# One more block's index scores in the projection, the attention's order rebuilt on them, split waits between the two stages, and a combination finished by VectorE one tile later

## The chip, the cores and the metric

The kernel is one program on one core of a Trainium2 chip. The core has five engines that run their own instruction streams and meet at semaphores: TensorE (PE; its weight loads are shown apart as PEld), VectorE (DVE), ScalarE (ACT), GpSimd (POOL) and SyncE (SP, which here only issues DMAs). The metric is the device time of one execution in microseconds (us).

## The reference

A decoder layer on 2048 tokens of width 1024, all in float32. Cut to what the change touches:

```python
h = layer_norm(x)
proj = h @ w_in                       # u, q (6 heads), k, v (2 heads), iq (8 index heads), ik, iw
# attention, in blocks of 128 queries
s = einsum('bqhd,bsd->bqhs', iq_block, ik)
idx_score = einsum('bqhs,bqh->bqs', relu(s), iw_block * w_scale)   # then causal
sel = top_k(idx_score, 256)           # softmax attention over the selected keys only
h = layer_norm(ALPHA_RES * h + concat(pool_out, attn_out) @ w_out)
# 32 experts, 4 per token; y are the experts' rows, tok and gates say whose they are
out = zeros.at[tok].add(y * gates)
h = layer_norm(ALPHA_RES * h + out)
```

Block b may see (b + 1) * 128 keys, so the top 256 are a real choice from block 2 on.

## The kernel before

Five stages follow each other, each a block of five instruction streams with a meeting of all engines at its end: projection, attention, placing of tokens on experts, experts, combination.

**Projection** (`project_stage`) walks 16 tiles of 128 tokens. TensorE does 40 matrix products a tile (L527) and, between them, transposes. For the blocks in `SEARCHED` = 2 to 6 it also makes the index scores: two matmuls for a pair of index heads (L498), `rectify` on ScalarE, a weighting matmul (L511), for each chunk of 512 keys. `schedule` says in which tile a block is scored (`score_at` = 3, 4, 6, 8, 11). VectorE then finds the limit of the 256 largest scores by 32 halvings (`search`, a "bit" is one pass L426 over the scores and two small instructions) and makes a mask, which goes to DRAM. ScalarE ends each tile by issuing three DMAs: `qi` (L564), `iw` (L567) and a sixteenth of the zeros that clear the spare rows of `y` (L570). At the end ScalarE waits for the stores of `qi`, `iw` and for `s_clear`, all sixteen clears.

**Attention** (`attend_stage`) walks the 16 blocks in the order `ORDER`, cut into `PHASES`. While the blocks of phase p are worked, VectorE searches block `SEARCHED[p]` (32 bits spread over the heads by `bits`, then `select`), and TensorE and ScalarE make the scores of the next one to be searched, one chunk of 512 keys in a slot (`at_slot`: step, head). Before, the phases were `(0,1,2,3), (4,15), (5,14), (6,13), (12,), (11,), (10,), (9,), (8,), (7,)` and the blocks to be searched 15, 14, 13, ..., 8, 7. Step 0 (block 0) had the four score chunks of block 15 and no search; the search began in step 1. Step 13 (block 9) had the two chunks of block 7, step 14 (block 8) its search, and step 15 (block 7) no search. `walk` sets one order of pieces for every engine: `logits`, `search`, `fill` (score and exponentials), `values`, and work of the two blocks before (`project`, `norm`, `route`, `choose`, `rank`, `scatter`). A block of up to 1024 keys uses half of the `qk` bank (`halved`), so two heads can be under way; a larger one the whole. VectorE and ScalarE began by waiting for all constants (`s_const`, nine DMAs) and, like TensorE, VectorE for all that GpSimd prepares (`s_made` 3).

**Combination** (`combine_stage`) walks 16 tiles. GpSimd gathers the four expert rows of each token with four indirect DMAs a tile (L2051), four tiles ahead (`rows` has four slots). TensorE adds them (L2091 the biases, L2098 the rows) in one of three banks, VectorE adds the residual and takes mean and variance (`sums`: L2126, L2129, L2130, L2132, L2134), GpSimd raises to the power -1/2 (L2068) and makes the shift in two more instructions (L2070, L2072), with a `drain` (wait until the engine's earlier work is done) between them. ScalarE applies scale and shift (L2158), and VectorE multiplies and adds (`affine`: L2139, L2141) one tile later. SyncE stores the tile; `total` has three slots.

Of the kernel before, what the change touches and what calls it, by code (L numbers as in the profile page):

```python
# [27 lines left out]
P = 128  # L28
# [47 lines left out]
def project_stage(nc, A, S, D_):  # L76
# [7 lines left out]
    SHARE = (MAX_VISITS - EXPERTS) * ROWS // TILES  # L84
    SHARE_N = next(n for n in range(1, SHARE + 1) if SHARE % n == 0 and SHARE // n <= P)
    assert SHARE * TILES == (MAX_VISITS - EXPERTS) * ROWS
# [3 lines left out]
    s_keys = [P * (b + 1) for b in SEARCHED]  # L90
    chunks = [-(-n // BANK) for n in s_keys]
    chunk0 = [sum(chunks[:s]) for s in range(len(SEARCHED) + 1)]

    def schedule():
# [4 lines left out]
        for s, b in enumerate(SEARCHED):  # L99
# [48 lines left out]
    with ExitStack() as ctx:  # L148
# [29 lines left out]
        bit_value = sb("bit_value_e", [P, 32])  # L178
        bit_next = sb("bit_next_e", [P, 32], I32)
        scores = sb("scores_e", [P, 2, EARLY * P])  # L180
        mask = sb("mask_e", [P, 2, EARLY * P], BF16)
        causal = sb("causal_e", [P, TOPK // P, TOPK], BF16)
# [3 lines left out]
        same_row = sb("same_row_e", [P, CUT])  # L186
# [23 lines left out]
        s_qst = [sem("p_qst0"), sem("p_qst1")]  # L210
        s_iwst = [sem("p_iwst0"), sem("p_iwst1")]
# [13 lines left out]
        with nc.Block() as block:  # L225
            @block.sync
            def _(sp):
# [7 lines left out]
                def load_queries(s):  # L235
                    b = SEARCHED[s]
# [32 lines left out]
                for b in range(TOPK // P):  # L269
                    sp.dma_start(D_["mask"][b * P:(b + 1) * P, 0:(b + 1) * P], causal[:, b, 0:(b + 1) * P]  # L270
                                 ).then_inc(s_early, 16)
# [22 lines left out]
            def _(pool):  # L294
# [9 lines left out]
                def cut(s):  # L304
                    b = SEARCHED[s]
# [13 lines left out]
                nc.gpsimd.memset(causal[:], 0.0)  # L319
# [9 lines left out]
                for b in range(TOPK // P):  # L329
                    op = nc.gpsimd.affine_select(out=causal[:, b], in_=causal[:, b], compare_op=ALU.is_ge, fill=NEG,  # L330
                                                 base=b * P, pattern=[[-1, TOPK]], channel_multiplier=1)
# [139 lines left out]
            def _(pe):  # L471
# [16 lines left out]
                def index(s, c, i):  # L488
# [3 lines left out]
                    if c == 0 and i == 0:  # L492
                        pe.wait_ge(s_iq, 16 * (s + 1))
                        pe.wait_ge(s_qi, 4 * SEARCHED[s] + 4)
# [43 lines left out]
            def _(act):  # L538
# [6 lines left out]
                def out_of_q(t, g):  # L545
# [15 lines left out]
                    else:  # L561
# [5 lines left out]
                        nc.scalar.dma_start(D_["iw"][t * P:(t + 1) * P, :], iw_now[:, slot]).then_inc(s_iwst[slot], 16)  # L567
                        shape = [SHARE // SHARE_N, SHARE_N * D // P, P]
# [59 lines left out]
                for n in range(2):  # L628
                    act.wait_ge(s_qst[n], 8 * TILES)
                    act.wait_ge(s_iwst[n], 8 * TILES)  # L630
                act.wait_ge(s_clear, 16 * TILES)


def attend_stage(nc, A, S, D_):
# [7 lines left out]
    CONSTS = 16 * 9  # L642
# [7 lines left out]
    PHASES = ((0, 1, 2, 3), (4, 15), (5, 14), (6, 13), (12,), (11,), (10,), (9,), (8,), (7,))  # L650
    SEARCHED = tuple(b for blocks in PHASES for b in blocks if b >= EARLY)
    ORDER = tuple(b for blocks in PHASES for b in blocks)
# [6 lines left out]
    chunks = [-(-n // BANK) for n in s_keys]  # L659
# [4 lines left out]
    for c in range(chunks[0]):  # L664
        at_slot[0, (1, 2, 4, 5)[c]] = (0, c)
    for s in range(1, N_SEARCH):
        steps = [k for k in range(TILES) if PHASE[k] == s - 1 and (s > 1 or k >= 2)]
# [5 lines left out]
    def bits():  # L673
# [3 lines left out]
        for s in range(N_SEARCH):  # L677
            slots = [(k, i) for k in range(TILES) if PHASE[k] == s and (s > 0 or k >= 1) for i in range(HEADS)]
# [19 lines left out]
    def walk(do):  # L698
# [29 lines left out]
        for k in range(TILES + 2):  # L728
# [27 lines left out]
            for s in range(1, N_SEARCH):  # L756
# [8 lines left out]
    with ExitStack() as ctx:  # L765
# [17 lines left out]
        scores = [sb("scores_even", [P, SEQ]), sb("scores_odd", [P, SEQ - P])]  # L783

        band0 = scores[1][:, 0:POOL_GROUPS * P].rearrange("p (g n) -> p g n", n=P)
# [4 lines left out]
        same_row = sb("same_row", [P, CUT])  # L790
# [22 lines left out]
        bit_value = sb("bit_value_sb", [P, 32])  # L813
        bit_next = sb("bit_next_sb", [P, 32], I32)
# [1424 lines left out]
```

## Time and profile before

| | us |
|---|---|
| median of 3 runs (5124.47 to 5127.0) | 5126.84 |
| the profiled execution's own time | 5125.14 |
| its span, first to last instruction | 5123.5 |
| projection, to the first instruction of attention | 602.13 |
| first instruction of the combination | 4888.58 |

TensorE's mean granted clock was 0.933 of full speed. Over the span TensorE was busy 4555.4 us (89%), VectorE 3081.0 (60%), ScalarE 1839.5 (36%), GpSimd 883.7 (17%). How to read the rows below: times are from the start of the span; a line L12 is line 12 of the kernel before; "[9.1 <-X]" is the time the engine stood idle before the instruction and what ended the wait; "issue" there means that no engine or transfer that the profile knows ended it.

### The profile page before, as it was taken

To read this page: it belongs to the slowest core of one execution; us is meant where nothing else is said; L and a number is where in the kernel's file an instruction comes from. 1 tells how busy PE (TensorE), PEld (TensorE's weight loads), DVE (VectorE), ACT (ScalarE), POOL (GpSimd) and SP (SyncE) were. 2 spreads that over 40 slices of the span, in tenths; PEclk is the share of its full clock that TensorE was granted. 3 is DMA by queue.
4 is the path that set the end of the run, shared out by engine and by line. 5 is a ranking of instruction groups with operands and counts; after the bars stand their busy time and mean duration, and the time that the engine had idled before them with its cause. 6 is when DMAs were issued, how large, how long until landed. Compare 5 with 4: busy or idle time off the path is not lost. (4 is left out here: it accounts for less than half of the span.)

```text
span 5123.5 us, 67487 instructions
## 1 busy us (share of the span) xinstructions
PE 4555.4 (89%) x23642; PEld 3404.9 (66%) x23695; DVE 3081.0 (60%) x4864; ACT 1839.5 (36%) x2652; POOL 883.7 (17%) x907
## 2 busy tenths in 40 slices
PE   8999777788888887489999999999999999999953
PEld 4444333344444444289999999999999999999920
DVE  3667445666678885365656655565675566765634
ACT  1222123233333332144444534353454444543411
POOL 0000012111111112221211221121121112211133
PEclk9999788999999898699999999999999999999965
DMA  4323400000000000255454644464565455654465
GB/s 165 122 92 119 135 18 25 16 18 23 12 18 14 21 14 14 99 192 181 176 176 174 227 160 170 161 215 170 174 225 190 164 198 180 220 190 177 141 224 192
DMA packets 523786, 666.09 MB, mean 130 GB/s; under 512 B 57920, under 2 KB 388160, under 8 KB 523616
## 3 DMA queue, kind: packets, MB, share of 16 engines
q1 hardware_dynamic: 400080, 484.90, 27.9%
q10 hardware_dynamic: 96992, 93.93, 5.4%
q0 software_dynamic: 26576, 85.56, 4.6%
q8 instruction: 69, 1.13, 0.1%
q14 instruction: 69, 0.57, 0.0%
HBM read 543.96 MB, written 120.36 MB: 130 GB/s over the span
## 5 line engine op out<-in xcount | busy, mean ns | idle before, releaser
L1767 PE MATMUL gu<-x_hi,w_hi 128*128 128x256 f32 (+2 forms) x4096 | 1229.8, 300 | 1.3 <-DVE x_lo L1849 1.3
L1768 PE MATMUL gu<-x_lo,w_hi 128*128 128x256 f32 (+2 forms) x4096 | 1229.6, 300 | 0.0
L1769 PE MATMUL gu<-x_hi,w_lo 128*128 128x256 f32 (+2 forms) x4096 | 1228.0, 300 | 0.0
L1844 DVE TENSOR_TENSOR w_lo<-w_raw,w_hi 128x2048 fp32r<-128x2048 f32 x386 | 874.6, 2287 | 530.8 <-ACT w_hi L1918 530.8
L1918 ACT ACTIVATE w_hi<-w_raw 128x2048 fp32r<-128x2048 f32 x386 | 726.8, 1907 | 280.6 <-PE gu L1769 198.7
L1767 PEld LDWEIGHTS gu<-x_hi,w_hi 128*128 128x128 f32 x4096 | 770.5, 188 | 2.5 <-issue 1.7
L1769 PEld LDWEIGHTS gu<-x_hi,w_lo 128*128 128x128 f32 x4096 | 771.4, 188 | 0.0
L1768 PEld LDWEIGHTS gu<-x_lo,w_hi 128*128 128x128 f32 x4096 | 769.4, 188 | 0.7
L1740 POOL TENSOR_TENSOR a_lo<-up,a_hi 128x384 fp32r<-128x384 f32 x256 | 396.8, 1550 | 1486.9 <-ACT a_hi L1930 1486.9
L1767 PE MATMUL yp<-w_hi,a_hi 128*128 128x512 f32 x1296 | 526.0, 406 | 0.0
L1768 PE MATMUL yp<-w_lo,a_hi 128*128 128x512 f32 x1296 | 514.8, 397 | 0.0
L1769 PE MATMUL yp<-w_hi,a_lo 128*128 128x512 f32 x1296 | 514.6, 397 | 0.0
L527 PE MATMUL proj_acc<-w_in_sb,hT 128*128 128x512 f32 (+1 forms) x1280 | 494.1, 534 | 0.7 <-ACT hT L543 0.7
L1855 DVE TENSOR_SCALAR gate<-gu,b_gu 128x384 f32<-128x384 f32 x256 | 157.5, 615 | 370.8 <-PE gu L1769 370.8
L1124 DVE TENSOR_REDUCE small<-qk 128x1 f32<-128x128 f32 (+15 forms) x96 | 123.9, 1291 | 404.9 <-PE qk L1265 338.0
L527 PEld LDWEIGHTS proj_acc<-w_in_sb,hT 128*128 128x128 f32 x1280 | 214.7, 191 | 215.2 <-issue 210.2
L1263 PE MATMUL qk<-kT,q_blk 128*128 128x512 f32 (+3 forms) x480 | 252.6, 612 | 58.0 <-ACT probs L1393 32.0
L1093 DVE TENSOR_SCALAR_CACHE_REDUCE mask<-scores_even,small 128x2048 bf16<-128x2048 f32 (+4 forms) x160 | 289.7, 1810 | 11.5 <-issue 0.5
L1769 PEld LDWEIGHTS yp<-w_hi,a_lo 128*128 128x128 f32 x1296 | 244.6, 189 | 59.4
L1767 PEld LDWEIGHTS yp<-w_hi,a_hi 128*128 128x128 f32 x1296 | 245.2, 189 | 55.4
L1768 PEld LDWEIGHTS yp<-w_lo,a_hi 128*128 128x128 f32 x1296 | 245.6, 189 | 52.7
L1288 PE MATMUL o_acc<-probsT,v_sb 128*128 128x384 f32 x544 | 246.9, 542 | 33.1 <-ACT probsT L1406 33.0
(287 smaller groups left out, 5400.8 us busy)
## 6 DMA issues: line engine op xcount, KB each, us to landing
w_raw<-w_gate_up SPq DMA_DIRECT2D x258, 1024.0 KB, 7.1
w_raw<-w_down SPq DMA_DIRECT2D x128, 1024.0 KB, 6.1
y_dram<-y_rows ACTq DMA_DIRECT2D x192, 256.0 KB, 2.6
y_dram<-zeros ACTq DMA_DIRECT2D x16, 2016.0 KB
h_blk<-h_dram SPq DMA_DIRECT2D x32, 512.0 KB, 7.2
qi_dram<-qi_stage ACTq DMA_DIRECT2D x16, 640.0 KB, 3.1
x_in<-x SPq DMA_DIRECT2D x16, 512.0 KB, 4.6
w_in_sb<-w_in SPq DMA_DIRECT2D x4, 2048.0 KB, 14.1
```

The lines of the kernel that those rows point to most:

```text
L527: mm = nc.tensor.matmul(acc[:, (5 * t + n) % ACCS, 0:width], hT[:, t % 2, k], w_in[:, k, c0:c0 + width], start=(k == 0), stop=(k == KD - 1))
L1093: nc.vector.tensor_scalar(reach, row, limit, 0.0, ALU.is_ge, ALU.add, accum_out=n_reach)
L1124: nc.vector.tensor_reduce(row_max[i % 2], qk_of(k, i), AX, ALU.max)
L1263: nc.tensor.matmul(out[:, at:at + width], q[:, k % 2, i], S["kT"][:, i // REP, at:at + width], start=True, stop=False)
L1288: nc.tensor.matmul(o_acc[:].rearrange("p a b -> p (a b)"), S["v"][:, c - 1, g * HEAD:(g + 1) * HEAD], probsT[:, (v0 + c - 1) % 2].rearrang ...
L1740: nc.gpsimd.tensor_tensor(a_lo[:, j], up[:, j % 2], a_hi[:, j].bitcast(F32), ALU.subtract).then_inc(s_al, 1)
L1767: nc.tensor.matmul(out, s_hi_, m_hi, start=(n == 0), stop=False)
L1768: nc.tensor.matmul(out, s_hi_, m_lo, start=False, stop=False)
L1769: op = nc.tensor.matmul(out, s_lo_, m_hi, start=False, stop=(n == len(pairs) - 1))
L1844: nc.vector.tensor_tensor(w_lo[:, c % 2, cols], raw[:, c % 3, cols], w_hi[:, c % 2, cols].bitcast(F32), ALU.subtract).then_inc(s_lo, 1)
L1855: nc.vector.tensor_scalar(g, gu[:, j % 2, 0, 0:ROWS], S["b_gu"][:, j, bass.ds(e, 1)], LIMIT, ALU.add, ALU.min).then_inc(s_gm, 1)
L1918: nc.scalar.activation(w_hi[:, c % 2, cols], raw[:, c % 3, cols], ACT.Copy).then_inc(s_hi, 1)
```

## The change

1. `SCORED` = `SEARCHED` + block 7 in the projection: block 7's scores (two chunks of 512 keys) are made in tile 13 and stay in a shared tile `scores`, where attention's first search finds them.
2. Attention's phases become `(0,1,2), (3,7), (4,15), (5,14), (6,13), (12,), (11,), (10,), (9,), (8,)`; block 7 is searched first, in steps 0 to 2, while block 15's four chunks are made there. The last step is block 8.
3. The clears of `y` are issued in 12 tiles instead of 16, a third larger each. The wait for the `qi` and `iw` stores leaves the end of the projection; attention's loads wait for the parts that they need (`qi_stored`, `iw_stored`).
4. Attention's opening waits are split: TensorE starts after GpSimd's first instruction, VectorE has no opening wait, ScalarE waits for the constants in its first `pool`. `bit_value`, `bit_next` and `same_row` are shared with the projection and no longer loaded or made again.
5. In the combination GpSimd only raises to the power; scale and shift move from ScalarE to one VectorE instruction in `finish`, one tile later.

Core of the diff:

```diff
-    SHARE = (MAX_VISITS - EXPERTS) * ROWS // TILES
+    CLEARS = 12
+    SHARE = (MAX_VISITS - EXPERTS) * ROWS // CLEARS
...
     SEARCHED = tuple(range(TOPK // P, EARLY))
-    s_keys = [P * (b + 1) for b in SEARCHED]
+    SCORED = SEARCHED + (EARLY,)
+    s_keys = [P * (b + 1) for b in SCORED]
...
             score_at.append(at)
+            if b not in SEARCHED:
+                break
...
+                        if t >= CLEARS:
+                            return
...
-                for n in range(2):
-                    act.wait_ge(s_qst[n], 8 * TILES)
-                    act.wait_ge(s_iwst[n], 8 * TILES)
-                act.wait_ge(s_clear, 16 * TILES)
+                act.wait_ge(s_clear, 16 * CLEARS)
...
-    PHASES = ((0, 1, 2, 3), (4, 15), (5, 14), (6, 13), (12,), (11,), (10,), (9,), (8,), (7,))
+    PHASES = ((0, 1, 2), (3, 7), (4, 15), (5, 14), (6, 13), (12,), (11,), (10,), (9,), (8,))
...
-    chunks = [-(-n // BANK) for n in s_keys]
+    chunks = [0] + [-(-n // BANK) for n in s_keys[1:]]
...
                 def load_iq(s):
                     b = SEARCHED[s]
-                    if s:
+                    if s > 1:
                         sp.wait_ge(s_idx, IDX_H * chunk0[s])
+                    else:
+                        for n in range(2):
+                            sp.wait_ge(S["qi_stored"][n], 8 * TILES)
...
+                nc.gpsimd.tensor_copy(ident_bf[:], S["ident"][:]).then_inc(s_made, 1)
                 nc.gpsimd.memset(w_pool[:], 0.0).then_inc(s_made, 1)
+                nc.gpsimd.memset(res[:], 0.0).then_inc(s_made, 1)
...
-                dve.wait_ge(s_const, CONSTS)
-                dve.wait_ge(s_made, 3)
...
-                pe.wait_ge(s_made, 3)
+                pe.wait_ge(s_made, 1)
...
                     pool.wait_ge(s_var, t + 1)
-                    nc.gpsimd.tensor_tensor(rstd, var_eps, minus_half[:], ALU.pow)
-                    pool.drain()
-                    nc.gpsimd.tensor_tensor(shift, mean, rstd, ALU.mult)
-                    pool.drain()
-                    nc.gpsimd.tensor_scalar(shift, shift, -1.0, 1.0, ALU.mult, ALU.mult).then_inc(s_rstd, 1)
+                    nc.gpsimd.tensor_tensor(rstd, var_eps, minus_half[:], ALU.pow).then_inc(s_rstd, 1)
...
-                def affine(t):
+                def finish(t):
                     slot = t % OUTS
-                    dve.wait_ge(s_norm, t + 1)
+                    dve.wait_ge(s_rstd, t + 1)
+                    nc.vector.tensor_scalar(total[:, slot], total[:, slot], small[:, slot, 12:13], small[:, slot, 15:16],
+                                            ALU.subtract, ALU.mult)
+                    dve.drain()
                     nc.vector.tensor_tensor(total[:, slot], total[:, slot], gain[:], ALU.mult)
```

GpSimd's stream in the combination, a turn or two of its loop before (`rows` are the gathers, `small` the statistics of one tile):

```order
L2051 DMA rows<-y_dram,pos_by_pick 128x1024 x4
L2068 TENSOR_TENSOR small<-small,minus_half 128x1
L2070 TENSOR_TENSOR small<-small 128x1
L2072 TENSOR_SCALAR small<-small 128x1
L2051 DMA rows<-y_dram,pos_by_pick 128x1024 x4
L2068 TENSOR_TENSOR small<-small,minus_half 128x1
```

and in the change, where the next tile's gathers stand right behind the power:

```order
L2049 DMA rows<-y_dram,pos_by_pick 128x1024 x4
L2066 TENSOR_TENSOR small<-small,minus_half 128x1
L2049 DMA rows<-y_dram,pos_by_pick 128x1024 x4
L2066 TENSOR_TENSOR small<-small,minus_half 128x1
L2049 DMA rows<-y_dram,pos_by_pick 128x1024 x4
```

The two instructions L2070 and L2072 and the drains before them are gone.

VectorE's stream at the start of attention before (`qk` holds a head's logits; the first three of step 0's six row maxima):

```order
L410 COPY rot<-rot 128x64
L225 UNCONDITIONAL_BRANCH
L1080 UNCONDITIONAL_BRANCH
L1124 TENSOR_REDUCE small<-qk 128x1
L1127 TENSOR_SCALAR small<-small 128x1
L1124 TENSOR_REDUCE small<-qk 128x1
L1127 TENSOR_SCALAR small<-small 128x1
L1124 TENSOR_REDUCE small<-qk 128x1
```

and in the change, where block 7's first bits stand between the row maxima of step 0:

```order
L1121 TENSOR_REDUCE small<-qk 128x1
L1124 TENSOR_SCALAR small<-small 128x1
L1086 MEMSET small 128x1
L1090 TENSOR_SCALAR mask,small<-scores,small 128x1024
L1092 SCALAR_TENSOR_TENSOR small<-small,bit_value_sb 128x1
L1095 SCALAR_TENSOR_TENSOR small<-small,bit_next_sb 128x1
L1090 TENSOR_SCALAR mask,small<-scores,small 128x1024
L1092 SCALAR_TENSOR_TENSOR small<-small,bit_value_sb 128x1
L1095 SCALAR_TENSOR_TENSOR small<-small,bit_next_sb 128x1
L1121 TENSOR_REDUCE small<-qk 128x1
```

The first search has moved from step 1 to step 0, and its passes are over 1024 keys instead of 2048.

TensorE's stream in tile 13 of the projection had, before, only products (`proj_acc`) and transposes (`proj_tr`); in the change the index matmuls (`pair_e`) and weightings (`total_e`) of block 7's first chunk stand there, and the second chunk's follow in the same way:

```order
L500 MATMUL pair_e<-ikT,iq_e 128x512 x2
L529 MATMUL proj_acc<-w_in_sb,hT 128x512 x2
L478 MATMUL proj_tr<-ident,x_in 128x128 x4
L500 MATMUL pair_e<-ikT,iq_e 128x512 x2
L529 MATMUL proj_acc<-w_in_sb,hT 128x512 x2
L500 MATMUL pair_e<-ikT,iq_e 128x512 x2
L529 MATMUL proj_acc<-w_in_sb,hT 128x512 x2
L478 MATMUL proj_tr<-ident,x_in 128x128 x4
L513 MATMUL total_e<-relu_e,w_sum_e 32x512 x4
L500 MATMUL pair_e<-ikT,iq_e 128x512 x2
```

Sixteen index matmuls and sixteen weightings have come into that tile, and as many have left step 13 of attention.

## Rows read from the trace of the kernel before

**Rows 1.** Chain that ended last and timeline, one tile of the combination: start, us, engine, line.

```profile
4977.83 1.04 POOL L2051 DMA_INDIRECT rows<-y_dram,pos_by_pick  x1 [0.49 <-issue]
4979.17 1.52 POOL L2051 DMA_INDIRECT rows<-y_dram,pos_by_pick  x1 [0.30 <-issue]
...
4983.84 7.87 issue
...
4991.49 3.42 PE L2098 MATMUL c_acc<-rows,g_sum 128*32 128x512 f32 x16 [7.15 <-DMA rows<-y_dram,pos_by_pick]
...
4992.78 1.05 POOL L2051 DMA_INDIRECT rows<-y_dram,pos_by_pick  x1 [0.49 <-issue]
```

**Rows 2.** Timeline, GpSimd: the first gather behind the opening sixteen.

```profile
4923.87 0.94 POOL L2051 DMA_INDIRECT rows<-y_dram,pos_by_pick  x1 [11.20 <-issue]
```

**Rows 3.** DMA view of 4890 to 5124: GB/s in 40 slices of 5.85 us.

```profile
GB/s 326 401 420 415 422 101 289 78 277 253 125 390 76 278 209 125 379 54 279 240 116 386 56 262 256 105 339 109 252 275 108 361 69 214 324 1 107 117 119 108
```

**Rows 4.** Timeline, VectorE: two tiles near the end, and a normalization in the projection.

```profile
26.38 0.81 DVE L380 TENSOR_SCALAR x_in<-x_in,small 128x1024 f32<-128x1024 f32 x1 [0.69 <-POOL small L313]
...
5099.85 1.22 DVE L2126 SCALAR_TENSOR_TENSOR total<-h_blk,c_acc 128x1024 f32<-128x1024 f32 x1
...
5105.31 1.21 DVE L2126 SCALAR_TENSOR_TENSOR total<-h_blk,c_acc 128x1024 f32<-128x1024 f32 x1
```

**Rows 5.** Timeline, ScalarE: one row a projection tile, scored tile first.

```profile
422.95 0.28 ACT L562 ACTIVATE ikT<-proj_tr 128x128 f32<-128x128 f32 x1 [1.23 <-PE proj_tr L484]
...
469.82 0.28 ACT L562 ACTIVATE ikT<-proj_tr 128x128 f32<-128x128 f32 x1 [1.23 <-PE proj_tr L484]
...
501.38 0.28 ACT L562 ACTIVATE ikT<-proj_tr 128x128 f32<-128x128 f32 x1 [1.23 <-PE proj_tr L484]
```

**Rows 6.** Timeline between the stages: ScalarE, SyncE, TensorE.

```profile
591.80 1.01 ACTq L570 DMA_DIRECT2D y_dram<-zeros  x1
...
602.13 0.32 SPq L912 DMA_DIRECT2D q_blk<-qi_dram  x1
...
606.82 0.58 PE L1263 MATMUL qk<-kT,q_blk 128*128 128x128 f32 x1 [15.90 <-POOL before L1011]
```

**Rows 7.** Waits, 585 to 625: who waited for whom, total, times, longest.

```profile
DVE small L1124 <- DMA w_pool_sb<-w_pool: 32.8, 1, 32.8
```

**Rows 8.** Timeline, VectorE: first row maximum of attention's steps 0-5, 8, 9, 14, 15.

```profile
617.48 0.29 DVE L1124 TENSOR_REDUCE small<-qk 128x1 f32<-128x128 f32 x1 [32.81 <-DMA w_pool_sb<-w_pool]
...
691.69 0.42 DVE L1124 TENSOR_REDUCE small<-qk 128x1 f32<-128x256 f32 x1 [9.35 <-PE qk L1265]
...
739.02 0.56 DVE L1124 TENSOR_REDUCE small<-qk 128x1 f32<-128x384 f32 x1 [4.51 <-PE qk L1265]
...
822.82 0.69 DVE L1124 TENSOR_REDUCE small<-qk 128x1 f32<-128x512 f32 x1 [5.11 <-remote]
...
906.05 0.82 DVE L1124 TENSOR_REDUCE small<-qk 128x1 f32<-128x640 f32 x1 [4.16 <-PE qk L1265]
...
987.68 2.29 DVE L1124 TENSOR_REDUCE small<-qk 128x1 f32<-128x2048 f32 x1 [7.94 <-PE qk L1265]
...
1292.48 1.09 DVE L1124 TENSOR_REDUCE small<-qk 128x1 f32<-128x896 f32 x1 [6.16 <-PE qk L1265]
...
1376.96 2.02 DVE L1124 TENSOR_REDUCE small<-qk 128x1 f32<-128x1792 f32 x1 [6.00 <-PE qk L1265]
...
1905.79 1.36 DVE L1124 TENSOR_REDUCE small<-qk 128x1 f32<-128x1152 f32 x1 [2.85 <-PE qk L1265]
...
2000.26 1.23 DVE L1124 TENSOR_REDUCE small<-qk 128x1 f32<-128x1024 f32 x1 [4.79 <-PE qk L1265]
```

**Rows 9.** Groups by line and form, and timeline: passes of 2048 and of 1024 keys.

```profile
L1093 DVE TENSOR_SCALAR_CACHE_REDUCE mask<-scores_even,small 128x2048 bf16<-128x2048 f32 x32 | 74.9, 2342 | 1.8
...
1909.38 1.28 DVE L1093 TENSOR_SCALAR_CACHE_REDUCE mask<-scores_even,small 128x1024 bf16<-128x1024 f32 x1
...
1911.29 1.28 DVE L1093 TENSOR_SCALAR_CACHE_REDUCE mask<-scores_even,small 128x1024 bf16<-128x1024 f32 x1
```

More of the change, by code:

```diff
@@ L98, in schedule @@
         now, left = 0, SLICE
-        for s, b in enumerate(SEARCHED):
+        for s, b in enumerate(SCORED):
             at = max(b + 1 if chunks[s] == 1 else b + 2, done_at[s - 2] + 1 if s >= 2 else 0,
@@ L318, in _ @@
                 nc.gpsimd.memset(same_row[:], 0.0)
-                nc.gpsimd.memset(causal[:], 0.0)
+                for b in range(TOPK // P):
+                    nc.gpsimd.memset(causal[b][:], 0.0)
                 pool.drain()
@@ L663, in attend_stage @@
     at_slot = {}
-    for c in range(chunks[0]):
-        at_slot[0, (1, 2, 4, 5)[c]] = (0, c)
     for s in range(1, N_SEARCH):
-        steps = [k for k in range(TILES) if PHASE[k] == s - 1 and (s > 1 or k >= 2)]
+        steps = [k for k in range(TILES) if PHASE[k] == s - 1]
         free = [(k, i) for i in (1, 4, 2, 5) for k in steps][:chunks[s]]
@@ L677, in bits @@
         for s in range(N_SEARCH):
-            slots = [(k, i) for k in range(TILES) if PHASE[k] == s and (s > 0 or k >= 1) for i in range(HEADS)]
+            slots = [(k, i) for k in range(TILES) if PHASE[k] == s for i in range(HEADS)]
             work = []
@@ L755, in walk @@
             fill(k, 5)
-            for s in range(1, N_SEARCH):
+            for s in range(2, N_SEARCH):
                 if slot_of[s - 1, chunks[s - 1] - 1][0] == k:
@@ L782, in attend_stage @@
         h = sb("h_blk", [P, D])
-        scores = [sb("scores_even", [P, SEQ]), sb("scores_odd", [P, SEQ - P])]
-        band0 = scores[1][:, 0:POOL_GROUPS * P].rearrange("p (g n) -> p g n", n=P)
+        scores_odd = sb("scores_odd", [P, SEQ])
+        scores = [(scores_odd if s % 2 else S["scores"])[:, 0:s_keys[s]] for s in range(N_SEARCH)]
+        scores[0] = S["scores"][:, SEQ // 2 * (EARLY % 2):SEQ // 2 * (EARLY % 2) + s_keys[0]]
+        band0 = S["scores"][:, 0:POOL_GROUPS * P].rearrange("p (g n) -> p g n", n=P)
         mask = sb("mask", [P, 2, SEQ], BF16)
@@ L911, in load_q @@
                     wait(sp, s_qk, HEADS * (k - 1))
+                    sp.wait_ge(S["qi_stored"][b % 2], 8 * TILES if k > 1 else 16 * (b // 2 + 1))
                     sp.dma_start(q[:, k % 2], D_["qi"][b * P:(b + 1) * P, 0:HEADS * P].rearrange(
@@ L926, in _ @@
                 load_mask(0)
-                load_iq(0)
+                load_iq(1)
+                for n in range(2):
+                    sp.wait_ge(S["iw_stored"][n], 8 * TILES)
                 for c in range(IDX_H // 2):
@@ L977, in after @@
                         load_mask(k + 1)
-                    for s in range(1, N_SEARCH):
+                    for s in range(2, N_SEARCH):
                         if slot_of[s - 1, chunks[s - 1] - 1][0] == k:
@@ L1087, in search @@
                     if first == 0:
-                        dve.wait_ge(s_causal, s + 1)
+                        wait(dve, s_causal, s)
                         nc.vector.memset(limit, 0.0)
                         dve.drain()
-                    row, reach = scores[s % 2][:, 0:s_keys[s]], mask[:, s % 2, 0:s_keys[s]]
+                    row, reach = scores[s], mask[:, s % 2, 0:s_keys[s]]
                     for i in range(first, last):
@@ L1102, in select @@
                 def select(n):
[L1104 removed]
+                    s, m = scores[n], mask[:, n % 2, 0:s_keys[n]]
                     nc.vector.tensor_scalar(m, s, limit, 0.0, ALU.is_gt, ALU.add, accum_out=n_reach)
@@ L2000, in combine_stage @@
         total = sb("total", [P, OUTS, D])
-        small = sb("small2", [P, OUTS, 17])
+        small = sb("small2", [P, OUTS, 16])
         minus_half = sb("minus_half2", [P, 1])
@@ L2063, in _ @@
                     slot = t % OUTS
-                    mean, var_eps, rstd, shift = (small[:, slot, j:j + 1] for j in (12, 14, 15, 16))
+                    var_eps, rstd = small[:, slot, 14:15], small[:, slot, 15:16]
                     if t + AHEAD < TILES:
@@ L2154, in _ @@
                                          ).then_inc(s_bts, 1)
-                for t in range(TILES):
-                    slot = t % OUTS
-                    act.wait_ge(s_rstd, t + 1)
-                    nc.scalar.activation(total[:, slot], total[:, slot], ACT.Identity, bias=small[:, slot, 16:17],
-                                         scale=small[:, slot, 15:16]).then_inc(s_norm, 1)
 def build(nc, A, upto=9):
@@ L2187, in build @@
             S["u"] = sb2("u_sb", [P, TILES, POOL_W])
+            S["scores"] = sb2("scores", [P, SEQ])
+            S["bit_value"] = sb2("bit_value_sb", [P, 32])
+            S["bit_next"] = sb2("bit_next_sb", [P, 32], I32)
+            S["same_row"] = sb2("same_row", [P, 2 * P // IDX_H])
+            S["qi_stored"] = [c2.enter_context(nc.semaphore(f"qi_stored{n}")) for n in range(2)]
+            S["iw_stored"] = [c2.enter_context(nc.semaphore(f"iw_stored{n}")) for n in range(2)]
             project_stage(nc, A, S, D_)
```

71 lines of the change are left out of this document (29 added, 42 removed).

## The prediction

> **What bounds the kernel now.** I read the chain that ended last first, then the timeline of the stages the change touches. The chain names the combination alone: from 4889 us on it is GpSimd. One turn of its loop lasts 14.95 us, from 4977.83 to 4992.78 [rows 1]. Four gathers and the power take 6.0 of them, to 4983.84. Then the engine stands 7.87 us in "issue" before L2070, that is in the drain behind the power. The drain ends at 4991.71, and TensorE's wait for the gathered rows ends 0.22 us before that, at 4991.49: the drain waits until the gathers just issued have landed. So every turn is issue plus landing, one after the other, and four slots of `rows` are of no use: TensorE waits 7.15 us for rows that were gathered in the same turn. The same shows behind the opening sixteen gathers, where GpSimd waits 11.20 us [rows 2].
>
> The transfers aren't the limit. In the first five slices, where sixteen gathers are issued without a drain between them, 326 to 422 GB/s move; afterwards slices of 390 alternate with slices of 54 to 125 [rows 3]. VectorE isn't either: freed of waits at the end it does a tile in 5.46 us [rows 4].
>
> The projection is bound by TensorE: a plain tile takes 31.56 us (469.82 to 501.38), a scored one 46.87 [rows 5]. Between the stages nothing works: ScalarE issues its last clear at 591.80, attention's first load is issued at 602.13, TensorE starts at 606.82 [rows 6], and VectorE's first row maximum comes at 617.48, after 32.8 us of waiting that the last constant's landing ended [rows 7]. Step 0 of attention then runs 74.2 us with no search [rows 8].
>
> **The combination, minus 83 us.** The change takes two small instructions and both drains from GpSimd's turn and ScalarE's 128x1024 pass from the path. What stays behind each other on GpSimd is four gathers and a power, 6.0 us [rows 1]. VectorE gets one more pass: the same form took 0.81 us in the projection, so its tile becomes 5.46 + 0.9 = 6.4 us [rows 4]. A tile moves four gathers of 128 rows of 4 KB, a load and a store of 0.52 MB each, 3.15 MB; at 420 GB/s [rows 3] that is 7.5 us. New waits: VectorE waits for the power of the tile before, with the next `sums` queued behind it, and the power stands behind four gathers (5.4 us), during which VectorE has a `sums` to do; GpSimd waits for the variance, with the next gathers behind it, which have three tiles in hand.
>
> So a turn lies between 6.4 (VectorE alone) and 13.7 us (issue and landing in series, 4977.83 to 4991.49). Three engines and the transfers all need 6 to 7.5 us, so some of their jitter adds up; I take 8.0, near the transfers' rate, since the opening shows that rate kept up. The first gather of the loop stays at 4923.87 [rows 2], because the opening drain stays. Eleven turns later, at 5011.9, the last tile is gathered; its rows land 13.7 later; then come TensorE's 3.4 [rows 1], VectorE's 6.4, and some 5 for power and store (an estimate, 3 to 8). The end is 4923.9 + 88 + 13.7 + 15 = 5040.6, against 5123.5: minus 83. At 6.4 a turn it is minus 100, at 13.7 minus 20.
>
> [...] A gather issued beside VectorE's additions takes 1.52 us instead of 0.94 to 1.04 [rows 1]: something between them is shared. [...] The change moves one more pass to VectorE beside the gathers; worked out from rows, this is the first rival below.
>
> **The projection, plus 17.5.** Block 7's two chunks come into tile 13, where TensorE has no free time: block 6's 896 keys cost 46.87 - 31.56 = 15.3 us [rows 5], so 1024 cost 15.3 x 8/7 = 17.5 in proportion. Some of block 6's cost was start-up that doesn't grow, so 15.3 is the lower end and 17.5 the upper. What else moves there is hidden: SyncE loads block 7's queries in tile 13 behind a store of `h`, as it did for the others; VectorE gains slack. The clears, 12 of 4/3 the size, are issued by ScalarE (1.01 us for the last [rows 6]), which waits for TensorE most of each tile; without that cover, 12 times about a third of a microsecond, 4 us.
>
> **Between the stages, minus 19.7.** The clear at 591.80 isn't issued, and no store is waited for, so the first load goes out at about 592.1 instead of 602.13. TensorE starts 4.7 later (602.13 to 606.82: the load and the mask, if not GpSimd, whose part becomes shorter), at 596.8, and VectorE's first row maximum comes about 1 us later, at 597.8 instead of 617.48 (before the 17.5 are added). Lower end: 10, if the first step waits for something else as long as it now does for constants; upper end 21. The waits that are split: SyncE holds block 15's index queries until tile 15's store has landed, about 3 us, and with them the loads of `iw`, the constants and the weights queued behind; all of these start 10 us earlier, so nothing is later than now. ScalarE's wait for constants and those for GpSimd's fourth preparation now stand behind the first head's exponentials or later, tens of microseconds after these loads.
>
> **Attention's steps, minus 21.** From `bits` and `at_slot`, each new step is taken from the nearest row. A chunk costs about 17 us where nothing covers it (step 0, 74.2 less some 6, by four [rows 8]); a bit of 1024 keys 1.91 us, one of 2048 keys 1.91 + 2.34 - 1.28 = 2.97 [rows 9].
> - Step 0 (block 0, two chunks, nine bits): 74.2 - 34, and the four bits that no chunk covers, 7.6: 48.
> - Step 1 (block 1): 47.3, thirteen bits of 1.91 for nine of 2.97, minus 2, a chunk plus 17, two bits under it minus 4: 58.
> - Step 2 (block 2): 83.8, ten bits for fourteen, minus 22.5, a selection of seven short passes plus 9, one chunk less but bits uncovered, minus 11: 59.
> - Step 3 (block 3, sixteen bits, two chunks): step 4 of before, 81.6, plus two bits, less one key tile: 85.
> - Step 4 (block 7, sixteen bits, two chunks, selection): step 8 of before (block 6, the same without selection), 84.5, plus longer passes 4, a key tile 2, some 10 of a selection over 2048 keys: 100.
>
> These are 350 against the 288.6 of steps 0 to 3 (617.48 to 906.05). The following steps are blocks 4, 15, 5, ... 10, with the same searches and chunks as before. Step 14 of before, block 8 with block 7's search, is gone, minus 94.5 (1905.79 to 2000.26). Block 9's step loses its two chunks, but it is VectorE's, minus 1. The last step is block 8 instead of 7: over 1024 keys a head takes the whole bank, so heads no longer overlap, about 5 us on two or three heads, plus 13. Together 61.4 - 94.5 - 1 + 13 = -21. The bounds are minus 45, if the bits all lie under other work, and plus 10, if each of the five steps needs 6 us more.
>
> **Sum.** -83 + 17.5 - 19.7 - 21 = -106. On the profiled execution's 5125.1 that gives 5019; this execution lies 1.7 below the median of the runs shown, which I leave inside the range.
>
> **Rivals.**
> - *The gathers are slowed by VectorE* (5047). If the 4.5 us of a tile's four large passes (three of 1.22, one of 0.81) block GpSimd in full, its turn is 6.0 + 4.5 = 10.5, and the combination gains 55 instead of 83. For it: the 1.52 us. Against it: the other three gathers keep 0.94 to 1.04 while VectorE works.
> - *Attention gains nothing* (5050). Early steps hang on chains of short instructions, and the whole-bank step at the end costs more: plus 10 in place of minus 21. For it: step 1 took 47 us for 27 us of bits. Against it: VectorE has nothing to do in step 0 now.
> - *The wait only moves* (5082). If GpSimd can't issue a tile's gathers before the last ones have landed, the turn is 13.7. Against it: the opening sixteen, which move over 400 GB/s.
> - *Slower.* `total` has three slots, and `sums` of a tile waits for the store of three tiles before. If gathers in flight hold each store up for some 30 us, VectorE stops and with it the loop. To be slower by more than 10 us than now the end must pass 5157, a turn of 18.6 us, longer than today's with all its waiting; nothing in rows 3 points to it.
>
> **Chances.** The forecast has 0.60, gathers slowed 0.14, no gain in attention 0.15, the wait that moves 0.04, slower 0.02; 0.03 for both of the first two going wrong further, so that the gain is lost; 0.02 for a turn of 6.4 with attention at minus 45 (4978). The range 4980 to 5062 leaves out the wait that moves, the lost gain, and the best corner. A change of 0.2%, 10 us, is about what a measurement tells from none: faster 0.95, same 0.03, slower 0.02.
>
> **What would show it.** In the combination: no "issue" wait of 7 us behind the power, gathers of one tile beginning about 8 us after those of the one before, no 7 us wait of TensorE for rows in mid-stage, DMA slices steadily over 350 GB/s, the end about 150 us after its first gather. In the projection: the tile with block 7 some 17 us longer than a plain one. At the seam: first load within 2 us of ScalarE's last store, VectorE's first row maximum within 8. In attention: steps 0 to 4 within 30 us of 350. The prediction is wrong if gathers begin over 10 us apart, or if the steps add up to over 400.

## The result, and the profile after

The changed kernel takes 5036.85 us (median of 4 runs, 5029.91 to 5037.77) against 5126.92 us of the kernel before beside it: a ratio of 0.9822, 95% interval 0.9805 to 0.9839. The forecast was 5019. Within the profiled executions the gain is 87.7 us (5125.14 to 5037.48), where the steps had 106. By stages, from the timelines of the two (first row maximum: VectorE's first in attention; attention: from there to the first instruction of the placing):

| us | before | after | change | forecast |
|---|---|---|---|---|
| to the first row maximum (projection and seam) | 617.5 | 616.2 | -1.3 | -2.2 |
| attention | 1493.1 | 1489.4 | -3.7 | -21 |
| placing and experts | 2778.0 | 2781.5 | +3.5 | 0 |
| combination, from its first instruction | 234.9 | 148.5 | -86.4 | -83 |

**Projection.** ScalarE's row a tile, as [rows 5]; start, us, engine, line:

```profile
425.58 0.28 ACT L564 ACTIVATE ikT<-proj_tr 128x128 f32<-128x128 f32 x1 [1.23 <-PE proj_tr L486]
...
472.93 0.28 ACT L564 ACTIVATE ikT<-proj_tr 128x128 f32<-128x128 f32 x1 [1.23 <-PE proj_tr L486]
...
504.49 0.28 ACT L564 ACTIVATE ikT<-proj_tr 128x128 f32<-128x128 f32 x1 [1.23 <-PE proj_tr L486]
...
552.85 0.28 ACT L564 ACTIVATE ikT<-proj_tr 128x128 f32<-128x128 f32 x1 [1.23 <-PE proj_tr L486]
```

The plain tile keeps 31.56 us (472.93 to 504.49). The tile with block 7 takes 48.36 (504.49 to 552.85), 16.8 more than it did.

**Seam.** Timeline, ScalarE, SyncE, TensorE and VectorE, as [rows 6] and the first of [rows 8]:

```profile
610.42 0.33 ACTq L566 DMA_DIRECT2D qi_dram<-qi_stage  x1
610.78 0.44 ACTq L569 DMA_DIRECT2D iw_dram<-iw_now  x1
611.70 0.32 SPq L916 DMA_DIRECT2D q_blk<-qi_dram  x1
...
615.33 0.77 PE L1259 MATMUL qk<-kT,q_blk 128*128 128x128 f32 x2 [4.95 <-DMA mask_early<-mask_dram]
...
616.24 0.29 DVE L1121 TENSOR_REDUCE small<-qk 128x1 f32<-128x128 f32 x1 [11.66 <-PE qk L1261]
```

The first load follows the last store's issue in 0.9 us, and VectorE starts 4.5 us after it; its wait for `w_pool` [rows 7] is gone.

**Attention.** First row maxima of steps 1 to 5, 14 and 15 (timeline, VectorE), as [rows 8]:

```profile
668.17 0.42 DVE L1121 TENSOR_REDUCE small<-qk 128x1 f32<-128x256 f32 x1 [3.97 <-PE qk L1261]
...
730.78 0.56 DVE L1121 TENSOR_REDUCE small<-qk 128x1 f32<-128x384 f32 x1 [2.98 <-PE qk L1261]
...
801.31 0.69 DVE L1121 TENSOR_REDUCE small<-qk 128x1 f32<-128x512 f32 x1 [8.88 <-PE qk L1261]
...
886.05 1.22 DVE L1121 TENSOR_REDUCE small<-qk 128x1 f32<-128x1024 f32 x1 [6.55 <-PE qk L1261]
...
976.39 0.82 DVE L1121 TENSOR_REDUCE small<-qk 128x1 f32<-128x640 f32 x1 [4.64 <-PE qk L1261]
...
1886.88 1.49 DVE L1121 TENSOR_REDUCE small<-qk 128x1 f32<-128x1280 f32 x1 [3.11 <-PE qk L1261]
...
1988.52 1.36 DVE L1121 TENSOR_REDUCE small<-qk 128x1 f32<-128x1152 f32 x1 [4.68 <-PE qk L1261]
```

Steps 0 to 4 take 360.2 us (616.2 to 976.4). The nine steps after them, which are the same blocks with the same searches and chunks as steps 4 to 12 before, take 910.5 where they took 900.4.

**Combination.** DMA view of 4887 to 5036, GB/s in 40 slices of 3.72 us, as [rows 3]:

```profile
GB/s 206 312 401 418 417 420 419 420 264 24 329 337 289 376 367 418 420 416 413 421 420 421 419 419 422 419 419 421 419 422 417 418 420 419 400 64 141 0 141 141
```

After a dip to 24 and five slices of 289 to 376, the transfers move 413 to 422 GB/s without a break for nineteen slices. The gathers on GpSimd (timeline; the first behind the opening sixteen, one beside VectorE) and the end of the chain that ended last (start, us, what):

```profile
4922.12 0.94 POOL L2049 DMA_INDIRECT rows<-y_dram,pos_by_pick  x1 [10.97 <-issue]
...
4964.92 1.53 POOL L2049 DMA_INDIRECT rows<-y_dram,pos_by_pick  x1 [0.19 <-issue]
4966.76 0.94 POOL L2049 DMA_INDIRECT rows<-y_dram,pos_by_pick  x1 [0.31 <-issue]
```

```profile
4969.25 20.87 DMA rows<-y_dram,pos_by_pick
...
4990.17 3.76 PE c_acc L2092 x16
...
4994.21 0.98 POOL rows L2049
...
4998.31 20.85 DMA rows<-y_dram,pos_by_pick
...
5019.20 3.48 PE c_acc L2092 x16
```

The last tile's gathers are issued from 4994.21 to 4998.31, but its rows land 20.85 us later, at 5019.16, where GpSimd had nothing left to issue. The opening drain is still there (10.97 us before 4922.12), and the dip in the row of GB/s is its mark.

### The profile page after: what moved, and what is told of

Same layout as the page of the kernel before. It is cut to its first block and busy times, and to the rows that moved or that the text cites. A ratio compares the mean times of both kernels' runs of the same rounds, so it can differ in the third digit from the quotient of the medians.

```text
span 5035.6 us, 67493 instructions
## 1 busy us (share of the span) xinstructions
PE 4555.1 (90%) x23694; PEld 3404.2 (68%) x23695; DVE 3091.1 (61%) x4881; ACT 1819.6 (36%) x2636; POOL 877.7 (17%) x871
## 5 line engine op out<-in xcount | busy, mean ns | idle before, releaser
L1090 DVE TENSOR_SCALAR_CACHE_REDUCE mask<-scores,small 128x1024 bf16<-128x1024 f32 (+4 forms) x160 | 272.5, 1703 | 11.3 <-issue 0.8
```

Of the source, the lines that this page charges most:

```text
L1090: nc.vector.tensor_scalar(reach, row, limit, 0.0, ALU.is_ge, ALU.add, accum_out=n_reach)
```

## The experiments

The runs in one table. "First row" is VectorE's first row maximum; the stages are read as above. One execution of each was profiled.

| run | median us (runs) | ratio to before, 95% interval | first row | attention | combination |
|---|---|---|---|---|---|
| combo_only | 5040.32 (5) | 0.9841, 0.9827 to 0.9854 | 617.1 | 1487.0 | 148.0 |
| rest_only | 5114.29 (11) | 0.9974, 0.9965 to 0.9983 | 615.4 | 1484.6 | 237.2 |
| drain_back | 5062.44 (4) | 0.9882, 0.9867 to 0.9897 | 615.4 | 1477.8 | 184.5 |
| drain_first | 5015.56 (5) | 0.9786, 0.9773 to 0.9800 | 614.8 | 1483.2 | 140.9 |
| after_again | 5033.06 (5) | 0.9809, 0.9793 to 0.9826 | 614.3 | 1478.3 | 148.7 |
| seam_back | 5038.20 (5) | 0.9819, 0.9805 to 0.9833 | 633.7 | 1481.6 | 148.3 |
| scalar_kept | 5023.26 (1) | | 614.8 | 1475.5 | 149.4 |
| no_residual | 5015.92 (1) | | 614.4 | 1478.9 | 139.6 |
| no_affine | 5027.11 (1) | | 614.0 | 1488.2 | 141.8 |
| drain_first_14 | 5027.08 (5) | 0.9796, 0.9782 to 0.9809 | 623.2 | 1483.5 | 140.2 |
| six_last | 5014.62 (5) | 0.9781, 0.9768 to 0.9795 | 618.2 | 1480.5 | 139.5 |

Executions of one and the same kernel lie up to 22 us apart here (5115.07 to 5137.02 of the kernel before, beside `after_again`), so terms under 10 us are read from the stages, not from the medians.

### combo_only and rest_only: which part carries the gain

`combo_only` is the kernel before with `combine_stage` of the change, `rest_only` the change with `combine_stage` of before.

> The kernel before with the change's combination alone. Theory (from the two traces): the combination carries the whole gain, minus 86, so some 5040 us; the combination lasts about 149 us from its first gather, gathers' turns 6 to 7 us, rows landing at the rate of the transfers. Rival (the steps of the forecast): minus 83 here and minus 23 in the other parts; the two agree on this run to 3 us and differ in the next one. If the combination's gain needed the other parts, this run would be above 5060.

> The changed kernel with the combination of before: projection, seam and attention changed. Theory: these parts give almost nothing, minus 1.6 with the experts' jitter, 5 without it, so 5120 to 5126 us. Forecast's steps: plus 17.5, minus 19.7, minus 21, so 5103. It also repeats the trace of the changed attention: if the 5 us longer steps of blocks 5 and 14 are TensorE's granted clock in that one execution, they come back to 83 and 107 us, or sit in other steps; if they belong to the new order, they stay at 88 and 111.6.

The combination alone gives 84.7 us (5125.06 to 5040.32), all else 10.8 (5125.06 to 5114.29). The other parts give more than the first profile made me think and about half of the forecast's 23. The steps of blocks 5 and 14 stayed at 88.0 and 111.7 us in this execution.

### drain_back: is it the drain?

```diff
                     nc.gpsimd.tensor_tensor(rstd, var_eps, minus_half[:], ALU.pow).then_inc(s_rstd, 1)
+                    pool.drain()
```

> The changed kernel with one drain put back behind the power, so that the next tile's gathers are issued behind it. Theory: the drain waits until the gathers just issued have landed, so a turn is issue plus landing, about 14 us, and nearly all of the gain is lost: 5105 to 5125 us. Rival (the gain came from moving ScalarE's pass to VectorE and from the shorter chain behind the power): a drain of a 128x1 instruction costs some tenths of a microsecond a tile, and the time stays within 10 us of 5037.

Neither held: the combination takes 184.5 us, 36 more than the change and 50 less than before. GpSimd's, SyncE's and TensorE's rows of one turn (timeline):

```profile
4939.00 0.97 POOL L2049 DMA_INDIRECT rows<-y_dram,pos_by_pick  x1 [5.10 <-issue]
...
4943.72 0.58 POOL L2066 TENSOR_TENSOR small<-small,minus_half 128x1 f32<-128x1 f32 x1
...
4949.69 0.98 POOL L2049 DMA_INDIRECT rows<-y_dram,pos_by_pick  x1 [5.39 <-issue]
```

```profile
4947.79 0.34 SPq L2039 DMA_DIRECT2D out<-total  x1
4948.17 0.45 SPq L2027 DMA_DIRECT2D h_blk<-h_dram  x1
...
4948.80 3.64 PE L2093 MATMUL c_acc<-rows,g_sum 128*32 128x512 f32 x16 [3.35 <-DMA rows<-y_dram,pos_by_pick]
```

The drain does wait for the gathers issued before it (5.39 us in "issue", and TensorE's wait for the same rows ends at 4948.80), so the turn is 10.7 us. But the store and the next load of `h` go out during that wait, before the next gathers. In the kernel before they hung on what stood behind the drain; its rows of the same kind (timeline, GpSimd, VectorE, SyncE):

```profile
4976.79 0.18 POOL L2070 TENSOR_TENSOR small<-small 128x1 f32<-128x1 f32 x1 [7.83 <-issue]
...
4978.65 1.23 DVE L2139 TENSOR_TENSOR total<-total,gain 128x1024 f32<-128x1024 f32 x1 [9.34 <-ACT total L2158]
...
4981.20 0.34 SPq L2041 DMA_DIRECT2D out<-total  x1
```

There the shift, ScalarE's pass and VectorE's two passes follow the drain, so the store and the load are issued from 4981.20 on, among the four gathers [rows 1], and the rows land at 4991.49 only. Of the 4.3 us by which that turn is longer (14.95 to 10.7), 2.5 are the longer wait in the drain (7.87 to 5.39), 1.1 the second drain and the two small instructions (4991.71 to 4992.78), and 0.7 slower gathers. So 36 us of the 86 are what one drain ahead of the next gathers costs. The other 50 came with all the rest that stood behind the drain: in the shares of this one turn (an estimate) some 29 are the longer landing, 13 the second drain and the two instructions, and 8 the slower gathers. That the store and load among the gathers lengthen the landing is read from their place in these rows; it fits that their 1.05 MB take 2.5 us at 420 GB/s (an estimate from the rates above), but no run moved them alone.

### scalar_kept: is ScalarE's pass worth anything?

```diff
+                def shift(t):
+                    slot = t % OUTS
+                    dve.wait_ge(s_rstd, t + 1)
+                    nc.vector.tensor_scalar(small[:, slot, 16:17], small[:, slot, 12:13], small[:, slot, 15:16], -1.0,
+                                            ALU.mult, ALU.mult).then_inc(s_shift, 1)
...
+                    nc.scalar.activation(total[:, slot], total[:, slot], ACT.Identity, bias=small[:, slot, 16:17],
+                                         scale=small[:, slot, 15:16]).then_inc(s_norm, 1)
```

> The changed kernel with the 128x1024 scale and shift on ScalarE again, the shift made by VectorE, no drain on GpSimd. Theory (transfers set the combination's pace, and what stands behind the power matters only if it delays the next gathers, store or load): the combination lasts 148 to 152 us as in the change. Rival (of the 86 us, the 50 that a drain alone did not take back are ScalarE's pass): it lasts about 200 us.

149.4 us in the one execution, as in the change: the rival falls, the 50 us are not the pass as such. With no drain on GpSimd, the move of scale and shift to VectorE is worth nothing measurable. In the kernel before, the pass stood between the drain and the store; its part in that delay was not tried alone.

### no_residual and no_affine: what sets the pace now

`no_residual` leaves out `load(t + AHEAD)`, `no_affine` the two instructions behind the `tensor_scalar` of `finish`.

> The changed kernel with h loaded for the combination's first four tiles alone; the other twelve add those again, so the residual is left out of the computation there. 6.3 MB fewer move. Theory (transfers set the pace at 420 GB/s): minus 15 us in the combination, 133 to 135. Rival (GpSimd's issue, VectorE or the slots of rows set it, 6.4 us a tile): no more than 5 us less, 144 to 149.

> The changed kernel without the multiplication by the gain and the addition of the bias in the combination (that part of the computation is left out): VectorE's tile loses two passes of 1.22 us, from about 6.6 to 4.0 us. Theory (transfers set the pace, with GpSimd's issue close behind): only the tail and some jitter go, 2 to 6 us less, the combination lasts 142 to 146. Rival (VectorE sets the pace, or its passes hold the gathers up): 2.5 us a tile, 110 to 125 us with what the next bound allows.

12% of the bytes fewer (6.3 of 51.6 MB) give 8.9 us (148.5 to 139.6), less than the 15 expected; two passes of 1.23 us a tile fewer on VectorE give 6.7 us in all (148.5 to 141.8), close to what I expected, and not 2.5 a tile. The windows in mid-stage (us, busy of PE, PEld, DVE, ACT, POOL, clock, DMA share, GB/s) of the change and of `no_residual`:

```profile
4930.00:5010.00 80.00, 64.03 (x200) 15.45 (x200) 68.86 (x91) 0.00 (x0) 56.70 (x55) 0.59 1.02 407
```

```profile
4930.00:4990.00 60.00, 52.14 (x181) 13.02 (x180) 55.29 (x74) 0.00 (x0) 45.88 (x44) 0.66 1.00 401
```

With fewer bytes VectorE is busy 92% (55.29 of 60), with the transfers still at 401 GB/s. That VectorE is the next bound, and the reason why 15 were not to be had, is read from this window; no run relieved both. So the transfers set the pace in the change, and VectorE stands close behind at 86% (68.86 of 80).

### drain_first: the dip at the opening

```diff
+                nc.gpsimd.memset(minus_half[:], -0.5)
+                pool.drain()
                 pool.wait_ge(S["relayed"], 64)
                 gather(0)
                 for t in range(1, AHEAD):
                     gather(t)
-                nc.gpsimd.memset(minus_half[:], -0.5)
-                pool.drain()
```

> The changed kernel with the memset of minus one half and its drain ahead of the first gathers instead of behind the opening sixteen. Theory (transfers set the combination's pace): the dip to 264 and 24 GB/s and the slow slices after it go, some 8 us of transfer at 420 GB/s, and the end comes 6 to 9 us earlier: about 5029. Rival (GpSimd, VectorE or the slots of rows set the pace, the dip is caught up): no change, 5037. A second rival: all 11 us of the opening wait are gained, 5026.

The combination takes 140.9 us, 7.6 less, as the transfers' rate makes it. DMA view of its 4877.7 to 5018.6, GB/s in 40 slices:

```profile
GB/s 208 322 406 424 415 426 412 419 422 416 426 416 421 420 416 422 407 423 418 422 419 420 421 419 422 417 422 420 420 419 415 421 420 420 264 0 149 0 149 149
```

No dip is left. The rival of 11 us, the whole wait, falls: what counts is the lost transfer. The median came down further, to 5015.56; its interval and that of `after_again` touch, and the rest is execution-to-execution spread that I can't tell from a gain.

### after_again: what repeats

> The changed kernel once more, beside the other runs of this series. The combination lasts 148 to 149 us as in the first profile. Theory on attention: its steps of one and the same order differ by up to 12 us between executions, with TensorE's granted clock, so the end of attention lies anywhere in 2093 to 2106, and the time in 5015 to 5038. If the first profile's 2105.6 comes back to within 1 us, the length belongs to this program's order.

Combination and projection repeat to a microsecond; attention does not: 1478.3 us against 1489.4, ending at 2092.6 against 2105.6. The step of block 5 takes 82.4 us instead of 88.0. Windows of that step, and of 7 us inside it behind the score chunk, in the first profile and here (columns as above):

```profile
1171.70:1259.70 88.00, 71.44 (x255) 33.66 (x256) 50.73 (x93) 27.89 (x56) 14.16 (x18) 0.86 0.06 20
...
1199.00:1206.00 7.00, 5.93 (x17) 2.53 (x18) 0.00 (x0) 1.29 (x5) 0.25 (x1) 0.51 0.00 0
```

```profile
1158.10:1240.50 82.40, 66.30 (x268) 33.42 (x269) 51.87 (x94) 30.37 (x62) 13.60 (x17) 0.96 0.06 21
...
1192.60:1199.60 7.00, 5.18 (x25) 2.58 (x27) 2.34 (x5) 2.29 (x7) 0.25 (x1) 1.00 0.00 0
```

and the eight weighting matmuls at the start of that stretch (timeline, TensorE; first profile, then this one):

```profile
1194.70 1.06 PE L1221 MATMUL acc<-relu,w_sum 128*32 128x512 f32 x8
...
1199.27 1.94 PE L1221 MATMUL acc<-relu,w_sum 128*32 128x512 f32 x8 [1.17 <-ACT relu L1375]
```

```profile
1192.88 1.07 PE L1221 MATMUL acc<-relu,w_sum 128*32 128x512 f32 x8 [1.17 <-ACT relu L1375]
```

The work and the waits are the same (1.17 us for ScalarE's `relu` in both), but in the first profile the granted clock there is 0.51, the lower of the two levels (1.2 GHz), and here 1.00. Ahead of the fall TensorE had short groups of matmuls with gaps of 1.1 to 1.2 us between them; here it had the same gaps and did not fall. Over ten executions of this order attention took 1475.5 to 1489.4 us, mean 1482.1; the two of the order before took 1493.1 and 1487.0, mean 1490.0.

### seam_back: the waits and the clears

```diff
-    CLEARS = 12
+    CLEARS = 16
...
+                for n in range(2):
+                    act.wait_ge(s_qst[n], 8 * TILES)
+                    act.wait_ge(s_iwst[n], 8 * TILES)
...
-                pe.wait_ge(s_made, 1)
+                pe.wait_ge(s_made, 4)
...
+                dve.wait_ge(s_const, CONSTS)
+                dve.wait_ge(s_made, 4)
...
+                act.wait_ge(s_const, CONSTS)
```

> The changed kernel with the clears in sixteen tiles again, the wait for all stores at the end of the projection, and the opening waits of attention for all constants and all of GpSimd's preparations. Theory: VectorE's first row maximum comes 20 us later behind TensorE's end, and tiles 3, 4 and 11 of the projection go back to 38.57, 40.1 and 46.87 us, minus 2.9, so plus 17 in all: the first row maximum at 633. Rival (the first step waits for something else): half of it, 625.

The timeline of the seam, ScalarE, SyncE, VectorE:

```profile
607.97 1.01 ACTq L574 DMA_DIRECT2D y_dram<-zeros  x1
...
618.42 0.32 SPq L919 DMA_DIRECT2D q_blk<-qi_dram  x1
...
633.69 0.29 DVE L1124 TENSOR_REDUCE small<-qk 128x1 f32<-128x128 f32 x1 [32.86 <-DMA w_pool_sb<-w_pool]
```

The first row maximum comes at 633.7 as expected, 17 to 20 us later than the 614.0 to 616.2 of the runs with twelve clears and without these waits, with the old wait for `w_pool` back (32.86 us). Tiles 3 and 4 of the projection are at 38.57 and 40.06 us again. Behind it attention takes 1481.6 us, inside the 1475.5 to 1489.4 of the same order, so in the profiled execution nothing is given back later. The medians differ by 5 us only (5038.20 to 5033.06), within their spread, so it isn't shown that the whole gain of the seam reaches the end of the kernel.

### drain_first_14 and six_last: a better version?

`drain_first_14` is `drain_first` with `CLEARS = 14`; `six_last` adds to it:

```diff
-    PHASES = ((0, 1, 2), (3, 7), (4, 15), (5, 14), (6, 13), (12,), (11,), (10,), (9,), (8,))
+    PHASES = ((0, 1, 2), (3, 7), (4, 15), (5, 14), (13,), (12,), (11,), (10,), (9,), (8, 6))
```

> The changed kernel with the opening drain ahead of the first gathers and the clears in fourteen tiles instead of twelve. Theory: the combination lasts 141 us as with the drain alone moved; tiles 3 and 4 of the projection come down from 39.4 and 40.9 us towards 38.6 and 40.1, 1 us in all, and no store is waited for at the end of the projection; time 5015 to 5025. Rival: the last clear, issued two tiles later, is waited for again, and the first row maximum comes later than 615.

> As the last, with block 6 moved behind block 8 to the end of attention, so that the two last blocks, which have no search beside them, end on a smaller one, and block 13's step holds the whole search of block 12 and its four chunks. Theory: block 13's step becomes 20 us longer, block 6's step without search and chunks 25 us shorter, the end behind it some 15 shorter, so attention gains 10 to 20 us and the time is 5000 to 5010. Rival (VectorE's 32 bits and the four chunks do not lie beside each other in one step): block 13's step grows by over 35 us, and nothing is gained, 5015 to 5025.

Fourteen clears were a miss: tiles 3 and 4 take 44.39 and 44.04 us (40.04 and 44.20 in `six_last`) instead of 39.4 to 40.3 and 40.8 to 41.6, and the first row maximum comes at 623.2; the seam behind them is as before, so the clear is not waited for at the end, as the rival had it. In `six_last` the first row maxima of blocks 13, 12, 8 and 6 (timeline, VectorE) show where the order's gain went:

```profile
1371.53 2.02 DVE L1121 TENSOR_REDUCE small<-qk 128x1 f32<-128x1792 f32 x1 [8.47 <-PE qk L1261]
...
1499.38 1.89 DVE L1121 TENSOR_REDUCE small<-qk 128x1 f32<-128x1664 f32 x1 [5.62 <-PE qk L1261]
...
1928.84 1.36 DVE L1121 TENSOR_REDUCE small<-qk 128x1 f32<-128x1152 f32 x1 [4.60 <-PE qk L1261]
1995.82 1.09 DVE L1121 TENSOR_REDUCE small<-qk 128x1 f32<-128x896 f32 x1 [13.43 <-PE qk L1261]
```

Block 13's step grows to 127.9 us (1371.53 to 1499.38) from 98 to 102, 26 to 30 more, between the 20 of the expectation and the 35 of its rival; the steps of block 6 and block 8 together take 169.8 to the end at 2098.7 instead of about 202. Attention in all takes 1480.5, inside the 1475.5 to 1489.4 of the other order: nothing that can be told from none. `six_last` and `drain_first` are the fastest that ran, 0.9781 and 0.9786, and not told apart; both stand below the change's 0.9809 and 0.9822, by 12 us or more, of which the opening drain is 7.6 in the profile.

## Why the prediction was right, and where it was off

The main step held: GpSimd's drain behind the gathers bounded the combination, and without it the transfers do. The time lies 18 us above the forecast, inside its range, and of the 18.3 us missing in the profile attention has 17.3.

**The combination, -83: right, by two wrong sizes that cancel.** Turns were to be 8.0 us and the last rows to land 13.7 behind their first gather. Gathers run ahead at 6.55 us a tile (4922.12 to 4994.21, eleven turns), while the transfers deliver a tile every 7.26 us at the end (4990.17 to 5019.20, four tiles; 7.5 by bytes), so the last rows come 25.0 us behind their first gather. From the loop's first gather to the last rows it is 97.1 us, against 88 + 13.7 = 101.7; behind the rows come 16.4 us for 15. That the sum came out within 4 us is luck. I had taken issue and delivery for one pace; each slot of `rows` that is ahead only lengthens the queue. And the cause was half told: I put the whole turn down to the drain in front of the gathers, where one such drain costs 36 of the 86 (`drain_back`). The other 50 went with what else stood behind it: by one turn's rows, some 29 of them with the store and the load of `h` sent late among the gathers, which no run tried alone.

**The transfers' 420 GB/s, right.** The Trainium skill, page "SBUF — State Buffer", section "SBUF: two separate sides", puts the peak of the DMA side at about 436 GB/s; the trace agrees, with 413 to 422 in mid-stage.

**Gathers slowed by VectorE: fell in size, not in kind.** Rows of 1.5 us remain (4964.92): 8 of the 48 gathers of the loop are over 1.3, and the mean is 1.10. All eight began while a pass of `finish` ran, seven of them under the two passes that read two SBUF tiles, and each ended 0.81 to 0.86 us after that pass did. The gather of 1.52 us in [rows 1] does the same: it starts at 4979.17 under the pass shown above (4978.65, 1.23 us) and ends 0.81 after it. So such a gather waits out what is left of the pass. The other three gathers of that turn, which seemed to speak against the rival, began under no such pass or with 0.2 us of it left. In `no_affine`, without those two passes, none is over 1.3 and the mean is 1.00. Against the 0.94 of a gather that waits for nothing, the 1.10 make 0.6 us a tile and not 4.5, since most gathers begin outside such a pass or near its end. The Trainium skill, page "SBUF — State Buffer", section "SBUF: two separate sides", says that a VectorE instruction with two SBUF inputs that starts first keeps the shared ports for its whole length, and that a GpSimd instruction which reads SBUF is blocked until then. The trace agrees: the gathers read their row numbers (`pos_by_pick`) from SBUF, and they end 0.81 to 0.86 us behind the pass.

**The projection, +17.5: right** at 16.8 for the tile. Hidden, I said, was the rest, and that was 3 us off: with 12 larger clears tiles 3, 4 and 11 were 1.7, 0.8 and 0.5 us longer in the first profile, TensorE waiting for the index queries before its first index matmuls; with 16 they are not (`seam_back`).

**The seam, -19.7: right.** First load 0.9 us behind the last store, first row maximum 4.5 behind that; `seam_back` gives 19 back against `after_again`, both read at the first row maximum.

**Attention, -21: the step that was mis-sized.** It measured -3.7 in the first profile and -8 in the mean over ten executions. In means, by its own terms: steps 0 to 4 356.6 us for 350 (steps 0 to 2 were 4.6, 4.5 and 9.7 longer, block 7's 11 shorter); the steps after them +6.9 for 0; block 9 +0.9 for -1; the dropped step -94.3 for -94.5; the last +9.3 for +13. I take it that the early steps hang on short chains that my sum by bits and chunks underrated, as the rival "attention gains nothing" said; no run tried this. The rival's price of 5050 was too high: attention still gained 4 to 8 us where the rival had it lose 10, and the last step cost less than forecast, not more. The unchanged steps go with TensorE's granted clock, which my sum didn't have (block 14's step took 107.0 us at 0.94 before, 111.7 at 0.88 or 108.1 at 0.91 in the change). That the new order itself brings the lower clock stays open: ten executions of it against two of the other, and both orders show steps that differ by 3 to 6 us.

**Experts, +3.5**, not in the sum: 2750.0 to 2754.0 us over all runs with the code unchanged; the kernel before had the least.

## What to carry to other kernels

A drain on GpSimd behind indirect gathers waited for their landing in these runs (5 to 8 us behind four gathers, 11 behind sixteen), and all that stands behind it waits too: look not only at what the engine issues next but at the stores and loads that hang on its result. Once such a wait is gone, ask for the delivery rate apart from the issue rate; the transfer lost in the dip, over the measured GB/s, priced the move of the opening drain to a microsecond. Terms of a few microseconds summed over many steps need several executions of the same order, or they drown in the granted clock.

## What the runs showed of the hardware that was not expected

- The same instructions in the same order ran at two patterns of TensorE's granted clock: the steps of blocks 5, 14, 6 and 13 took 88.0, 111.7, 84.4, 98.2 us or 82.4, 108.1, 83.7, 102.2 (sums 382.3 and 376.4), five executions each and nothing between. In the order before, two executions took 372.8 and 372.1 for the same four steps.
- The size of a clear changed the tiles beside it in a way that bytes alone don't explain: tile 3 took 38.57 us with 504 rows in a clear (126 partitions of 4 rows), 39.4 to 40.3 with 672 (112 of 6), 44.39 and 40.04 with 576 (96 of 6). The loads of `x` landed in 4.7, 7.5 and 8.4 us (medians). That it is the number of partitions was not tested.
